# Retention's values in two halves, its queries and keys from a 512-column product, and four buffers for raw weights

## What is computed

```python
def second_block(...):                       # per layer l
    x = x + 0.5 * rmsnorm_2(swiglu(rmsnorm_2(x, ...), ffn1...), ...)
    x = x + rmsnorm_2(hybrid_mixer(rmsnorm_2(x, ...), ...), ...)
    x = x + 0.5 * rmsnorm_2(swiglu(rmsnorm_2(x, ...), ffn2...), ...)

def hybrid_mixer(u, ...):
    xa, ya, q, k, v, g, sb, sc, sh, gates = jnp.split(u @ w_in, cuts, axis=-1)
    oa = (rg_lru(causal_depthwise_conv(xa, ...), ...) * jax.nn.gelu(ya)) @ w_lru_out
    ret = retention(q, k, v, positions)      # 4 heads: 256 wide in q and k, 512 wide in v
    ob = (jax.nn.silu(g) * ret) @ w_ret_out
    oc = (sb * causal_depthwise_conv(sc * sh, ...)) @ w_sc_out
    ga, gb, gc = jnp.split(jax.nn.sigmoid(gates), 3, axis=-1)
    return (ga * oa + gb * ob + gc * oc) @ w_out
```

## Time and profile before

| | |
|---|---|
| median of 3 runs | 2328.06 us (2327.79 to 2328.37) |
| profiled execution | 2328.21 us |
| its span in the trace | 2326.4 us |
| granted TensorE clock, mean | 0.999 of 2.4 GHz |
| busy: PE / PEld / DVE / ACT / POOL | 2302.6 / 1956.3 / 1526.1 / 1227.6 / 71.7 us |
| weights and other loads | 434.90 MB, mean 187 GB/s |

### The profile page before, as it was taken

The page is one execution under the profiler, slowest core; times in us unless marked ns, Lnnn a source line. Parts: engine busy times, 40 slices in busy tenths (PEclk is TensorE's granted clock), DMA queues, the critical chain, the costliest instruction groups (busy, mean ns, idle before and its releaser), DMA issues.

```text
span 2326.4 us, 30308 instructions
## 1 busy us (share of the span) xinstructions
PE 2302.6 (99%) x12100; PEld 1956.3 (84%) x12100; DVE 1526.1 (66%) x1987; ACT 1227.6 (53%) x1788; POOL 71.7 (3%) x134
## 2 busy tenths in 40 slices
PE   8999999999999999999999999999999999999998
PEld 6888888888888888978888888888889788888887
DVE  6867567776566666866575665665667665756664
ACT  6645456464455556745444554555567553445553
POOL 0110000100000000000000000000000000000000
PEclk9999999999999999999999999999999999999999
DMA  8436656356656556645565466565556455654653
GB/s 297 145 118 222 210 174 224 127 159 214 210 166 220 182 179 195 206 158 181 181 198 193 153 216 197 177 220 187 174 196 213 152 181 182 192 197 163 197 193 126
DMA packets 119803, 434.90 MB, mean 187 GB/s; under 512 B 13552, under 2 KB 13808, under 8 KB 119664
## 3 DMA queue, kind: packets, MB, share of 16 engines
q1 hardware_dynamic: 119664, 432.96, 56.3%
HBM read 431.86 MB, written 1.05 MB: 186 GB/s over the span
## 4 chain that ended last, share of the span: by engine, by line
PE 90%; DVE 5%; DMA 2%; ACT 1%; POOL 1%; issue 1%; SPq 0%; DVEq 0%; POOLq 0%; ACTq 0%
PE ub L1669 21%; PE ub L1666 11%; PE ub L1637 9%; PE ub L1639 8%; PE ub L1638 8%; PE acc L1637 8%; PE acc L1638 8%; PE acc L1639 8%; DMA raw<-in_w 2%; PE ub L1644 1%; PE ub L1645 1%; PE ub L1646 1%; DVE wlo L992 1%; DVE XN L1033 1%; ACT junk L528 1%
## 5 line engine op out<-in xcount | busy, mean ns | idle before, releaser
L992 DVE TENSOR_TENSOR wlo<-raw,whi 128x1024 fp32r<-128x1024 f32 x776 | 915.9, 1220 | 259.2 <-ACT whi L506 257.1
L506 ACT ACTIVATE whi<-raw 128x1024 fp32r<-128x1024 f32 x776 | 783.4, 1053 | 259.4 <-PE ub L1639 141.6
L1669 PE MATMUL ub<-xhl,whi 128*128 128x512 f32 x2176 | 515.4, 391 | 0.0
L1669 PEld LDWEIGHTS ub<-xhl,whi 128*128 128x128 f32 x2176 | 404.2, 188 | 83.4 <-issue 2.3
L1637 PE MATMUL acc<-whi,bhl 128*128 128x512 f32 x736 | 288.2, 392 | 0.0
L1638 PE MATMUL acc<-wlo,bhl 128*128 128x512 f32 x736 | 286.7, 389 | 0.0
L1639 PE MATMUL acc<-whi,bhl 128*128 128x512 f32 x736 | 286.6, 389 | 0.0
L1637 PE MATMUL ub<-whi,xhl 128*128 128x512 f32 (+1 forms) x704 | 275.2, 391 | 5.7 <-DVE wlo L992 4.1
L1666 PEld LDWEIGHTS ub<-xhl,wlo 128*128 128x128 f32 x2176 | 272.1, 191 | 6.2
L1666 PE MATMUL ub<-xhl,wlo 128*128 128x256 f32 x2176 | 275.4, 283 | 0.0
L1639 PE MATMUL ub<-whi,xhl 128*128 128x512 f32 (+1 forms) x704 | 272.6, 387 | 0.0
(11 more groups left out here) (302 smaller groups left out, 2438.9 us busy)
## 6 DMA issues: line engine op xcount, KB each, us to landing
raw<-in_w SPq DMA_DIRECT2D x776, 512.0 KB, 4.9
gain<-in_gains SPq DMA_DIRECT2D x20, 512.0 KB, 7.9
tapw<-in_taps SPq DMA_DIRECT2D x16, 512.0 KB, 4.4
DEC<-in_decay SPq DMA_DIRECT2D x2, 768.0 KB, 7.6
par<-in_par SPq DMA_DIRECT2D x2, 647.0 KB, 7.6
par<-in_par SPq DMA_DIRECT2D x2, 556.0 KB, 7.1
H<-in_x SPq DMA_DIRECT2D x2, 512.0 KB, 4.4
out_h<-H SPq DMA_DIRECT2D x4, 256.0 KB, 2.6
```

What stands on the lines that cost most here:

```text
L506: do(act.activation(whi[:, s % RING, c], raw[:, s % RAW, c], ACT.Copy), counts["w_hi"])
L992: do(dve.tensor_tensor(wlo[:, s % RING, c], raw[:, s % RAW, c], whi[:, s % RING, c].bitcast(f32), ALU.subtract), counts["w_lo"])
L1669: last = pe.matmul(bank, whi[:, s % RING, n:n + P], xhl[:, kt, :, :].rearrange("p a n -> p (a n)"), start=first, stop=stop, skip_group_che ...
```

## The change

Four things are done.

1. **Values.** `V` becomes two tiles, `Vhi` (ScalarE's rounded copy, in V's place) and `Vlo` (VectorE: bank minus `Vhi`, `rest_of_v`, eight subtractions of 128 x 512 per layer). The scores times decays are split the same way into `SMhi` and `SMlo`: `decayed` is now three VectorE operations instead of one. `values` becomes nine one-pass products instead of three plain float32 ones.
2. **Queries and keys.** q and k chunks use `pair` instead of `tile`. ScalarE now copies half of the sums out for each (`sums_out`), VectorE adds the other half (`sums`), and then does the four operations that it did before, reading `tS` instead of the bank.
3. **Raw slots.** RAW is 4. `Vlo` lies in slots 2 and 3, so from v4 to the last chunk before sc0 the weights use slots 0 and 1 alone (`lent`, `PLACES`); SyncE waits for the last `values` before it loads sc0.
4. **Room.** The space kept at the start of each partition for dynamic DMA shrinks from 16 KB to 1 KB, which moves every tile's address.

```diff
-RAW = 2
+RAW = 4
+SCRATCH = 1024
...
+def lent(s):
+    n = s - LAYERS * B1["end"]
+    return n >= 0 and AT2["v", 4] <= n % len(ORDER2) < AT2["sc", 0]
+
+def places():
+    last, came, got = [-1] * RAW, [0] * RAW, []
+    for s in range(TOTAL):
+        slot = min(range(RAW // 2 if lent(s) else RAW), key=lambda n: last[n])
+        came[slot] += 1
+        got.append((slot, came[slot], last[slot]))
+        last[slot] = s
+    return got
...
                 def load(s, parts=(0, 1)):
+                    slot, _, before = PLACES[s]
                     for k in parts:
-                        n, c = 2 * s + k, slice(k * HALF, (k + 1) * HALF)
-                        if s >= RAW:
-                            sp.wait_ge(sem["w_lo"], n - 2 * RAW + 1)
...
+                        c = slice(k * HALF, (k + 1) * HALF)
+                        if before >= 0:
+                            sp.wait_ge(sem["w_lo"], 2 * before + k + 1)
...
+                        if s == s2(L, "sc", 0):
+                            sp.wait_ge(sem["pv2"], RET_HEADS * (L + 1))
...
-                        elif (kind, j) == ("q", 0):
+                        elif kind in ("q", "k"):
+                            slot = 0 if kind == "q" else 1
+                            if j:
+                                act.wait_ge(sem["qk_ready"], 8 * L + 2 * j - 1 + slot)
+                            else:
+                                act.wait_ge(sem["xs"], 4 * L + 3 + slot)
+                            sums_out(slot, s, slot)
+                        if (kind, j) == ("q", 0):
                             sigmoids(2)
...
-                            act.wait_ge(sem["xs"], 4 * L + 4)
+                            act.wait_ge(sem["qk_ready"], 8 * L + 8)
...
+                    def rest_of_v(vb, bank, t):
+                        nxt("vah")
+                        do(dve.tensor_tensor(Vlo[:, t, fcol(vb)], ub[:, bank, :], Vhi[:, t, fcol(vb)].bitcast(f32), ALU.subtract),
+                           counts["va"] if t else None)
...
-                        do(dve.tensor_tensor(SM[:, :], acc[:, 2, 0:RSPAN], DEC[:, hd * RSPAN:(hd + 1) * RSPAN], ALU.mult),
-                           counts["sm2"])
+                        weights = DEC[:, hd * RSPAN:(hd + 1) * RSPAN]
+                        do(dve.tensor_tensor(weights, acc[:, 2, 0:RSPAN], weights, ALU.mult))
+                        settle()
+                        do(dve.tensor_copy(SMhi[:, :], weights))
+                        settle()
+                        do(dve.tensor_tensor(SMlo[:, :], weights, SMhi[:, :].bitcast(f32), ALU.subtract), counts["sm2"])
...
                             dst, slot = (q2, 0) if kind == "q" else (k2, 1)
-                            used(s)
+                            both = units(tS[:, slot, :])
+                            sums(slot, slot, both, "pd")
                             settle()
-                            bank = units(ub[:, 2 * slot, :])
-                            do(dve.tensor_tensor(units(tX[:, 0, :]), bank, cos_sin, ALU.mult))
-                            do(dve.tensor_tensor(units(tX[:, 1, :]), bank, sin_cos, ALU.mult), counts["pd"])
+                            do(dve.tensor_tensor(units(tX[:, 0, :]), both, cos_sin, ALU.mult))
+                            do(dve.tensor_tensor(units(tX[:, 1, :]), both, sin_cos, ALU.mult))
...
-                        pe.matmul(acc[:, 0, :], SM[:, 0:P], V[:, 0, vs], start=True, stop=True)
-                        pe.matmul(acc[:, 1, :], SM[:, P:S], V[:, 0, vs], start=True, stop=False)
-                        give(pe.matmul(acc[:, 1, :], SM[:, S:RSPAN], V[:, 1, vs], start=False, stop=True), "pv2")
+                        for t, c0, tv in ((0, 0, 0), (1, P, 0), (1, S, 1)):
+                            o, w_hi, w_lo = acc[:, t, :], SMhi[:, c0:c0 + P], SMlo[:, c0:c0 + P]
+                            pe.matmul(o, w_hi, Vhi[:, tv, vs], start=c0 < S, stop=False, skip_group_check=True)
+                            pe.matmul(o, w_hi, Vlo[:, tv, vs], start=False, stop=False, skip_group_check=True)
+                            last = pe.matmul(o, w_lo, Vhi[:, tv, vs], start=False, stop=c0 != P, skip_group_check=True)
+                        give(last, "pv2")
```

More of the change, by code:

```diff
@@ L75 @@
 AT2 = {key: n for n, key in enumerate(ORDER2)}
+TOTAL = LAYERS * (B1["end"] + len(ORDER2))
+def lent(s):
[9 more added lines that the diff above has]
+    return got
+PLACES = places()
 FFN_AT = {(0, "f1"): 2, (0, "f2"): 3, (1, "f1"): 4, (1, "f2"): 5}
@@ L126, in build @@
     ACT, ALU, AX = mybir.ActivationFunctionType, mybir.AluOpType, mybir.AxisListType
-    TOTAL = LAYERS * (B1["end"] + B2["end"])
     with ExitStack() as ctx:
-        place = [16640]
+        place = [SCRATCH + 256]
         def sb(name, units, dtype=f32, at=None, shape=None):
@@ L141, in build @@
         UNIT = S * 4
+        raw_at = place[0]
         raw = sb("raw", 0, shape=[P, RAW, CHUNK])
@@ L157, in build @@
         gain = sb("gain", 0, shape=[P, 2, D])
+        cst_at = place[0]
         cst = sb("cst", 0, shape=[P, K["end"]])
@@ L228, in build @@
         DEC = sb("DEC", 0, at=free_at + P2["w_ax"] * 4, shape=[P, RET_HEADS * RSPAN])
-        SM = cst[:, K["rcount"]:K["rcount"] + RSPAN]
+        Vlo = sb("Vlo", 0, f32r, at=raw_at + RAW // 2 * CHUNK * 4, shape=[P, 2, 2048])
+        SMhi = sb("SMhi", 0, f32r, at=cst_at + K["rcount"] * 4, shape=[P, RSPAN])
+        SMlo = sb("SMlo", 0, f32r, shape=[P, RSPAN])
         Ag = sb("Ag", 8, at=unit(0))
         Rg = sb("Rg", 8, at=unit(8))
-        V = sb("V", 0, at=unit(16), shape=[P, 2, 2048])
+        Vhi = sb("Vhi", 0, f32r, at=unit(16), shape=[P, 2, 2048])
         Ig = sb("Ig", 8, at=unit(32))
@@ L504, in prep @@
                         c = slice(k * HALF, (k + 1) * HALF)
[L505 to L506 removed]
+                        slot, came, _ = PLACES[s]
+                        act.wait_ge(sem[f"w_in{2 * slot + k}"], 16 * came)
+                        do(act.activation(whi[:, s % RING, c], raw[:, slot, c], ACT.Copy), counts["w_hi"])
                         at[0] += 1
@@ L991, in lo @@
                         dve.wait_ge(sem["w_hi"], at[0] + 1)
-                        do(dve.tensor_tensor(wlo[:, s % RING, c], raw[:, s % RAW, c], whi[:, s % RING, c].bitcast(f32),
+                        do(dve.tensor_tensor(wlo[:, s % RING, c], raw[:, PLACES[s][0], c], whi[:, s % RING, c].bitcast(f32),
                                              ALU.subtract), counts["w_lo"])
@@ L1485, in _ @@
                     dve.wait_ge(sem["par_in"], 16 * (LAYERS + L + 1))
-                    lo(sv + 5)
+                    for vb in range(2):
+                        rest_of_v(vb, 2 * vb, 0)
+                    for vb in range(2):
+                        lo(sv + 4 + vb)
+                        rest_of_v(vb, 2 * vb + 1, 1)
                     for n, (kind, j) in enumerate(mix_order()):
@@ L1495, in _ @@
                         lo(s + 3)
-                        if kind == "xa":
+                        if kind == "v" and n > 3 and j % 2:
+                            for t in range(2):
+                                rest_of_v(j // 2, 2 + t, t)
+                        elif kind == "xa":
                             slot = (0, 0, 0, 1)[j]
@@ L2174, in _ @@
                         elif kind in ("q", "k"):
-                            slot = 0 if kind == "q" else 1
-                            fill(U_[2 * slot], "pd")
-                            for f in range(2):
-                                arrive(s, f)
-                                for kt in range(KT):
-                                    last = tile(ub[:, 2 * slot, f * S:(f + 1) * S], xhl[:, kt, :, :], s, f * KT + kt,
-                                                kt == 0, kt == KT - 1)
-                            give(last)
+                            pair(s, 0 if kind == "q" else 1, "pd")
                             if j == 0:
```

21 lines of the change are left out of this document (9 added, 12 removed).

## The result

| | before | changed kernel |
|---|---|---|
| median of the runs, us | 2328.07 (20 runs, 2327.48 to 2330.91) | 2332.21 (20 runs, 2331.53 to 2333.44) |
| ratio to before, 95% interval | | 1.0018 (1.0012 to 1.0024) |
| span of the profiled execution, us | 2326.4 | 2331.6 |

The kernel is 4.1 us slower. By the bound of 0.2% that is no change, but the interval excludes 1: the loss is real, and small.

The account below looks back on a forecast made before the run. TensorE bounds the kernel, busy 2302.6 of 2326.4 us, with VectorE nearly full from k1 to k3. Per layer +3.2, -2.1 and +1.0 make +2.1; two layers +4.2, less 0.4 for loads: 2332.0 us, 80% range 2324.5 to 2335.5.

Parts of the forecast that it names:

- TensorE's saving: Query/key chunks and values on TensorE: 0.19 us saved per chunk, 0.53 per head, together 7.2 us if no wait appears.
- the end would come 2.3 us later: By the skill's issue-gap figures, 16 chunks save 0.7 us in place of 3.0, ending 2.3 us later than forecast.
- The additions: VectorE, query and key chunks: 0.72 us each, five making 3.6 us, so k3's rotation ends at 997.8.
- Pieces at q3 and g0, about 2 us at the scores: TensorE waits for VectorE's additions at q3 or g0, then about 2 us at `scores2(0)`.
- The first values, +3.2 us: `values(0)` starts at 1005.3 instead of 1002.09, 7.5 us after k3's rotation, 3.2 us later than before.
- 1.0 us at the first transposes: At `turn_p(0)` TensorE waits about 1.0 us for VectorE's late `gated_values`.
- Four slots: Raw weight slots: TensorE's waits at the norms change by about 0, bounds 0 and -9.5; 0.4 us taken off.
- The sum: Per layer +3.2 to first values, -2.1 for values, +1.0 at first transposes: +2.1 us.
- The cover holds: VectorE's additions fit pauses or rotation runs quicker; TensorE keeps 7.2 us: 2321.0, or half, 2325 to 2328; chance 0.17.
- Four slots help: Weight waits at the norms go, -9.5 us at most, say -5, while VectorE eats the gain: 2327; chance 0.11.
- the fourth: ScalarE's bank copies wait for TensorE, delaying g0 to g2 weights and VectorE; 2 us per layer gives 2336; chance 0.07.

Follow-up runs that it names:

- e1: Changed kernel with query and key chunks read by `tile` as before, split values and four raw slots kept: 2323.74 us.
- e5: Kernel before with one more VectorE product, its result overwritten, per query and key chunk: 2333.23 us.
- e2: Kernel before with only `pair` for query and key chunks, VectorE's additions and ScalarE's wait for k3's rotation: 2334.14 us.
- e6: Changed kernel with ScalarE's wait for k3's rotation moved from ahead of the casts to just before the first Silu: 2330.01 us.
- e3: Kernel before with only the four raw slots and the smaller reserved DMA space: 2327.45 us.
- e11: Changed kernel, all eight pairs kept, VectorE's other work spread into pauses and behind the scores, ScalarE's wait at the first Silu: 2322.61 us.
- e4: Changed kernel with `pair` for q0, k0 and q1 alone, the other query and key chunks by `tile`: 2323.11 us.
- e7: Changed kernel with the 2.29 us product Ig x Cg moved from VectorE to GpSimd: 2330.39 us.
- e9: Changed kernel with the product Ig x Cg moved from VectorE to GpSimd in eight pieces of 128x256: 2329.07 us.

## Why the prediction was right

The forecast of 2332.0 us met 2332.21, and by its own steps. Two small errors stood against each other: the sum per layer was 0.4 us too low, and the medians lie 0.9 us closer together than the two layers' nets say.

- *TensorE's saving.* 0.19 us per chunk and 0.53 per head. Measured: 0.18 to 0.22 us per chunk, 1.6 per layer, and a head's values cost 0.48 less (e1: four heads, 1.92), since nine products take 2.10 us, 0.233 each, not 0.228. Together 7.0 us of saving, not 7.2. The chunk went by the trace's pitches. By the rule of the Trainium skill, "TensorE: Matmul & The Clock Gate", "Back-to-back issue gap", it would have been 0.04 us. That with this the end would come 2.3 us later was wrong by the prediction's own sum: there VectorE sets when the scores start, whatever the chunks save, and e5, whose chunks save nothing, nets 2.68 beside e2's 2.80.
- *The additions.* 0.72 us each on a full VectorE, five of them: right. They run at 0.72 to the next start. k3's rotation ended at 998.47, less the 0.54 us by which this execution came later to the mixer 997.9, where I had 997.8; e5 shows that this load is enough.
- *Pieces at q3 and g0, about 2 us at the scores.* Measured 0.82, 1.54 and 1.74 us. That the loss comes in pieces doesn't change the sum, which VectorE sets.
- *The first values, +3.2 us.* Measured +3.25 (1005.88 against 1002.09, less 0.54 of later start). The chain that I gave for it, with 7.5 us from the rotation to the split scores, took 1005.83 - 998.47 = 7.4, and e6 shows that 1.1 us of it is the new wait of ScalarE.
- *1.0 us at the first transposes.* Measured 0.76, and 0.28 more inside them.
- *Four slots.* Taken as -0.4 us between 0 and -9.5. e3 gives 0.6 less, with an interval from 2.8 less to 1.4 more. By the medians it isn't shown that this is more than 0; the traces show 0.1 to 0.4 us of it.
- *The sum.* +2.1 per layer; measured +2.5, because the values saved 0.2 less per layer and the values of head 0 gave back another 0.1 after their wait. Two layers make +5.0, the medians differ by 4.1 with an interval from 2.8 to 5.6: the 0.1 to 0.4 us that the slots save outside the mixer lie between them, and the rest is within the interval. So every term was near, and the last tenths of agreement are luck.
- *The rivals.* "The cover holds" failed as it was argued: no pause was there to take up the additions. e11 shows that it would have held with the same work in another order. "Four slots help" found next to no time to help with, the 0.1 to 0.4 us above. ScalarE was late, as the fourth had it, but at one place, behind its new wait, and its price was already in the forecast.

## What to carry to other kernels

When two engines are full in the same stretch, shortening the one by giving the other more work costs the other's whole duration, less what slack there is: 0.2 us of TensorE per chunk for 0.72 us of VectorE lost 5.6 us (e2). The same exchange ahead of the stretch, where VectorE still had pauses, gained 0.06 and 0.42 us per layer of the 0.6 that it could (e4). So before such an exchange look for work in the stretch that isn't wanted there: moving one product of 2.29 us per layer, with the order behind the scores changed to suit, gave 3.7 us back, and the order of e11 made the change as a whole a gain. And place a wait at the instruction that needs it: what was queued behind it was wanted 1.1 us sooner.

## What the runs showed of the hardware beyond that

- After a wait TensorE's next group is slower than the same group without one, though its clock is granted in full: 1.33 for 1.23 us for eight products of the scores (1.33 in e2 too), 2.21 for 2.10 for nine of the values. The 0.1 us lies between the starts of its first two products: 0.32 in place of 0.22 in the scores, 0.34 in place of 0.23 in the values. It isn't the length of the wait, since e4 shows it at q3 behind a wait of 0.05 us. It isn't the wait alone either: the first two products of k0 and of q1, which follow the gates, are 0.1 us further apart than the next ones without any wait. What it is stays open. Of the 0.28 us in the transposes, 0.17 is something else: their second half starts at 1016.30, right after VectorE's second half of the gated values, which ends at 1016.24.
- One GpSimd product of 128x2048 took 4.63 us, twice VectorE's 2.29, and VectorE's subtraction, begun 1.04 us after it, ended 3.46 us late (e7). In eight pieces GpSimd needed 8.69 us beside a busy VectorE (e9).
